# The order of the products in a blocked triangular inverse: both Y of a pair of steps, then both Z

## The reference, cut to what matters

```python
kb = k * beta[..., None]
a_mat = jnp.where(strict, jnp.einsum("bhnid,bhnjd->bhnij", kb, k) * decay, 0.0)
rhs = jnp.concatenate([v * beta[..., None], kb * jnp.exp(gc)[..., None]], axis=-1)
sol = lax.linalg.triangular_solve(a_mat + eye, rhs, left_side=True, lower=True,
                                  unit_diagonal=True)
...
def step(s, inp):
    u_n, w_n, qk_n, qd_n, kt_n, gt_n = inp
    v_new = u_n - jnp.einsum("bhck,bhkv->bhcv", w_n, s)
    o = jnp.einsum("bhck,bhkv->bhcv", qd_n, s) + jnp.einsum("bhcj,bhjv->bhcv", qk_n, v_new)
    s = s * gt_n[..., None, None] + jnp.einsum("bhck,bhcv->bhkv", kt_n, v_new)
    return s, o
```

## Time and profile before

| what | value |
|---|---|
| median of three executions | 3063.61 us |
| the profiled execution, its own time | 3054.48 us |
| its span, first to last instruction | 3052.8 us |
| mean granted TensorE clock, share of full speed | 0.939 |
| TensorE matmuls busy, over the span | 2665.8 us (87%) |
| VectorE / ScalarE / GpSimd busy | 1777.7 / 1232.9 / 1169.0 us |
| chunk stage, inverse and state, 1758 to 2742 us | 984 us |

### The profile page before, as it was taken

How to read it: one execution, slowest core, us unless ns; L and a number is a source line. 1 busy time by engine, 2 the same in 40 slices (tenths; PEclk the granted TensorE clock), 3 DMA queues, 4 the chain that set the end, 5 groups by cost and what they waited for, 6 DMA issues and landing times. The chain is left out here.

```text
span 3052.8 us, 52964 instructions
## 1 busy us (share of the span) xinstructions
PE 2665.8 (87%) x18657; PEld 2562.7 (84%) x18657; DVE 1777.7 (58%) x2689; ACT 1232.9 (40%) x2107; POOL 1169.0 (38%) x1110
## 2 busy tenths in 40 slices
PE   4799999984997299999999799999999999994994
PEld 3799999974996299999999799998998999994993
DVE  2266666666102357778777756766666666664004
ACT  2255555554112244444444434454554544443101
POOL 3333333322220134545444344455545455543220
PEclk9899999997998599999999889999999999997996
DMA  3111111113112035555554352424234243214103
GB/s 114 49 50 57 58 57 52 57 50 128 67 41 112 20 96 150 137 151 158 151 158 143 112 157 45 117 49 109 74 83 109 46 108 108 52 37 160 49 27 111
DMA packets 244802, 275.54 MB, mean 90 GB/s; under 512 B 86907, under 2 KB 210380, under 8 KB 242972
## 3 DMA queue, kind: packets, MB, share of 16 engines
q1 hardware_dynamic: 240028, 256.31, 29.5%
q10 hardware_dynamic: 4608, 17.04, 1.4%
HBM read 185.78 MB, written 87.53 MB: 90 GB/s over the span
## 5 line engine op out<-in xcount | busy, mean ns | idle before, releaser
L1895 ACT ACTIVATE zz<-ps 104x416 fp32r<-104x416 f32 x560 | 286.5, 518 | 379.8 <-PE ps L1786 378.4
L551 PE MATMUL ps<-dn_yhi,dn_whi 128*128 128x416 f32 (+1 forms) x1152 | 395.4, 343 | 18.5 <-POOL dn_wlo L535 13.1
L1958 DVE TENSOR_TENSOR pp<-ps,level_mask 104x416 fp32r<-104x416 f32 x560 | 318.3, 585 | 114.5 <-PE ps L1786 113.9
L552 PE MATMUL ps<-dn_ylo,dn_whi 128*128 128x416 f32 (+1 forms) x1152 | 376.1, 326 | 0.0
L553 PE MATMUL ps<-dn_yhi,dn_wlo 128*128 128x416 f32 (+1 forms) x1152 | 376.0, 326 | 0.0
L551 PE MATMUL ps<-rg_yhi,rg_whi 128*128 128x416 f32 (+1 forms) x768 | 256.2, 334 | 57.5 <-POOL rg_wlo L535 36.9
L1788 PE MATMUL ps<-pp,zz 104*104 104x208 f32 x1440 | 264.2, 293 | 18.4 <-DVE pp L1958 16.0
L552 PE MATMUL ps<-rg_ylo,rg_whi 128*128 128x416 f32 (+1 forms) x768 | 255.2, 332 | 0.0
L553 PE MATMUL ps<-rg_yhi,rg_wlo 128*128 128x416 f32 (+1 forms) x768 | 254.2, 331 | 0.0
L1788 PE MATMUL ps<-zz,pp 104*104 104x208 f32 x1440 | 245.1, 280 | 0.0
L551 PEld LDWEIGHTS ps<-dn_yhi,dn_whi 128*128 128x128 f32 x1152 | 218.9, 190 | 25.0 <-POOL dn_wlo L535 13.5
(11 more groups left out here) (283 smaller groups left out, 7311.3 us busy)
## 6 DMA issues: line engine op xcount, KB each, us to landing
c_nq<-nq_scratch SPq DMA_DIRECT2D x160, 169.0 KB
dn_raw<-in_dn_w_in SPq DMA_DIRECT2D x48, 512.0 KB, 4.0
qd<-rows_scratch SPq DMA_DIRECT2D x160, 104.0 KB, 3.3
rg_raw<-in_rg_w_in SPq DMA_DIRECT2D x32, 512.0 KB, 4.0
nq_scratch<-p_nq SPq DMA_DIRECT2D x48, 338.0 KB
p_ex<-rows_scratch SPq DMA_DIRECT2D x32, 422.5 KB
nq_scratch<-p_rn SPq DMA_DIRECT2D x32, 338.0 KB
o_scratch<-a SPq DMA_DIRECT2D x16, 520.0 KB, 2.8
```

What stands on the lines that cost most here:

```text
L551: e.matmul(o, whi, mhi[:, t0:t0 + tn], start=(first and k == 0), stop=False)
L552: e.matmul(o, whi, mlo[:, t0:t0 + tn], start=False, stop=False)
L1895: e.activation(zz[:, b, :, :], ps[0:CH, 2 * b + 1, 0:m4], ACT.Copy).then_inc(zev.sem, 1)
L1958: e.tensor_tensor(D4(pp[:, b, l % 2, :, :]), D4(Y4), c["level_mask"][:, l, :, 0:CH].unsqueeze(2).to_broadcast([CH, 2, 2, CH]), ALU.mult).t ...
```

## The change

In slots 1 to 7, TensorE no longer does Y and Z of the first step and then Y and Z of the second. The call for the first step does nothing; the call for the second does Y of both steps and then Z of both. What each group computes, where it reads and writes, what it waits for and which semaphore it raises are as before. Slots 0, 8 and 9 move into `ends` and keep their order. The other engines' programs are the same, and the counts of `ym` and `zm` come in the same order within each semaphore.

```diff
@@ dn_chunks, block.tensor, make(n)
                 def inverse(g, l):
-                    b, q4 = g % 2, g % 4
+                    if not 1 <= l <= LEVELS:
+                        ends(g, l)
+                    elif g % 2:
+                        for side in (grow_y, grow_z):
+                            side(g - 1, l)
+                            side(g, l)
+
+                def grow_y(g, l):
+                    b = g % 2
+                    old, p_ = nhr[:, g % 4] if l == 1 else zz[:, b], pp[:, b, (l - 1) % 2]
+                    e.wait_ge(yev.sem, yev.at(n, nth(g, l - 1, YS)))
+                    if l >= 2:
+                        e.wait_ge(zev.sem, zev.at(n, nth(g, l - 2, LEVELS)))
+                    for m in MS:
+                        ins = widened(2 * b, m, old[:, m, :], p_[:, m, :])
+                    ins.then_inc(ym.sem, 1)
+
+                def grow_z(g, l):
+                    b = g % 2
+                    old, p_ = nhr[:, g % 4] if l == 1 else zz[:, b], pp[:, b, (l - 1) % 2]
+                    if l == 1 and g >= 2:
+                        e.wait_ge(tb_done.sem, tb_done.at(n, g - 1))
+                    for m in MS:
+                        ins = widened(2 * b + 1, m, p_[:, m, :], old[:, m, :])
+                    ins.then_inc(zm.sem, 1)
+
+                def ends(g, l):
...
-                    elif l <= LEVELS:
-                        old, p_ = nhr[:, q4] if l == 1 else zz[:, b], pp[:, b, (l - 1) % 2]
-                        e.wait_ge(yev.sem, yev.at(n, nth(g, l - 1, YS)))
-                        if l >= 2:
-                            e.wait_ge(zev.sem, zev.at(n, nth(g, l - 2, LEVELS)))
-                        for m in MS:
-                            ins = widened(2 * b, m, old[:, m, :], p_[:, m, :])
-                        ins.then_inc(ym.sem, 1)
-                        if l == 1 and g >= 2:
-                            e.wait_ge(tb_done.sem, tb_done.at(n, g - 1))
-                        for m in MS:
-                            ins = widened(2 * b + 1, m, p_[:, m, :], old[:, m, :])
-                        ins.then_inc(zm.sem, 1)
```

More of the change, by code:

```diff
@@ L1799, in inverse @@
                         for m in MS:
-                            ins = widened(2 * b, m, nhr[:, q4, m, :], ident_r[:, :])
+                            ins = widened(2 * b, m, nhr[:, g % 4, m, :], ident_r[:, :])
                         ins.then_inc(ym.sem, 1)
-                    elif l <= LEVELS:
-                        old, p_ = nhr[:, q4] if l == 1 else zz[:, b], pp[:, b, (l - 1) % 2]
-                        e.wait_ge(yev.sem, yev.at(n, nth(g, l - 1, YS)))
-                        if l >= 2:
-                            e.wait_ge(zev.sem, zev.at(n, nth(g, l - 2, LEVELS)))
-                        for m in MS:
-                            ins = widened(2 * b, m, old[:, m, :], p_[:, m, :])
-                        ins.then_inc(ym.sem, 1)
-                        if l == 1 and g >= 2:
-                            e.wait_ge(tb_done.sem, tb_done.at(n, g - 1))
-                        for m in MS:
-                            ins = widened(2 * b + 1, m, p_[:, m, :], old[:, m, :])
-                        ins.then_inc(zm.sem, 1)
                     elif l == LEVELS + 1:
```

## The result

The changed kernel takes 3086.2 us in the median (3084.26 to 3090.51), the kernel before, beside it, 3061.31 us: a ratio of 1.0085, 95% interval 1.0068 to 1.0103, or **24.9 us slower**. The forecast was 3077.1, with 3072 to 3083 as its own range and 3066 to 3090 with the rivals. Two more comparisons gave 1.0076 (1.0060 to 1.0092) and 1.0102 (1.0073 to 1.0132). The profiled execution has 3085.98 us with a span of 3084.3.

What follows compares the result with a forecast made beforehand. TensorE's queue was taken to set the chunk stage's pace, with no slack in the zz loop. Terms 9.1 + 2.0 + 2.4 = 13.5 us, added to the median 3063.6, gave 3077.1 us; own range 3072 to 3083, with rivals 3066 to 3090.

Steps and rivals of the forecast that it cites:

- the clock rival: Added stops in the chunk stage tip four undisturbed table periods into lower clock: 12 us more, about 3089 us; chance 0.08.
- The loop Y0, Z0, eviction, Y0: TensorE to ScalarE and back: 1.15 us from Z0 to next Y0, no slack; a bare level grows from 1.55 to 1.93.
- 9.1 + 2.0: Boundary 4 to 5: 24 bare cases at 0.38 us, plus 40 at 0.05 for Y1 behind paired ScalarE evictions.
- The covers: TensorE's state pieces after levels 2, 3, 5 and 7, each over 0.43 us, hide the loss there.
- the 0.46 of L1878: L1878's matmuls, after level 1 in three periods of five and level 6 in two, just hide the loss.
- no gain on VectorE: Y1 reaches VectorE 0.38 us earlier, but rr waits for TensorE's state product after 0.70 idle, so zero gain.
- taken back: Rival: VectorE waits at 6 to 7 swallow most of the 4 to 5 loss, leaving 5.7 us (3069); chance 0.10.
- the pairs: Second of two successive evictions delays Y1 by 0.05 us: 2.0 us in all on ScalarE, 2.4 on VectorE.
- Periods 26.1 and 23.6: Sign: chunk-stage periods of 25.5 and 23.0 us become 26.1 and 23.6.
- Those with the square within 0.1: Sign: periods where ScalarE does the output's square (L1908) ahead of zz stay within 0.1 us.
- TensorE's waits for zz up by 9 to 11: Sign: the sum of TensorE's zz waits rises about 9 to 11 us, some written to the weight loads.
- Waits for VectorE near 31: Sign: TensorE's waits for VectorE, 28.9 us before, stay near 29 plus 2.

Runs made afterwards that it cites:

- Level 4 alone: Changed kernel with both Y before both Z kept only in level 4, other levels in the old order: 3070.26 us, 1.0035 against the kernel before.
- level 3 alone: Changed kernel with both Y before both Z kept only in level 3: 3057.21 us against 3059.25 for the kernel before, ratio 0.9995.
- levels 2, 3 and 5: Changed kernel with both Y before both Z kept only in levels 2, 3 and 5: 3072.12 us, ratio 1.0045 to the kernel before.
- late tables: VectorE's four table operations moved behind the inverse's slot 7: 3064.4 us on the changed kernel, 3047.8 in the old order, 3042.66 there with scalings later too.
- level 5 alone: Changed kernel with both Y before both Z kept only in level 5: 3073.7 us, ratio 1.0053 to the kernel before.

## Why the prediction was right, and where it was off

The direction and the mechanism were right, the size was not: 13.5 us were forecast and 24.9 measured. 3086.2 lies above the forecast's own range, which ends at 3083, and inside the wide one only because that reached up to the clock rival. Some 16 us are the forecast's mechanism; the rest is mostly clock, to which it gave 0.08.

**Right: the bound and the place.** The loop Y0, Z0, eviction, Y0 had no slack; with one more group in it the level at 4 to 5 is 1.93, as computed. Level 4 alone costs 10 us, where the sum had 9.1 + 2.0 for this boundary. The covers held: level 3 alone costs nothing, and the 0.46 of L1878 hid what it was to hide (A and B grow by 0.10 and 0.14, not by 0.4). What the prediction did not look at is the entry of a level: Y1, moved earlier, has its own bare side at 4 to 5, which levels 2, 3 and 5 showed. In the full change it falls on the same boundary, so the sum did not suffer; that was luck.

**Right: no gain on VectorE.** rr is released by the state product; the early Y evictions only lengthened the idle time ahead of it, from 0.70 to 0.99. The waits of 0.30 and 0.86 at 6 to 7 are 0.31 and 0.88 now, so nothing was taken back.

**Mis-sized: the pairs.** The offsets from the period's start, medians of the two traces, show the parts. In C, D and E, level 4 starts 0.09 later than before; levels 4 and 5 add 0.36 to 0.39; levels 6 and 7 add 0.11 to 0.13. So the second of a ScalarE pair cost next to nothing, not 0.05. The second of a VectorE pair cost 0.12 at 6 to 7, not 0.05: Y1 came 0.50 after Y0, where I had 0.47, and I had left out that the group after it takes 0.42 in place of 0.38. At the levels' start the same happens at 0 to 1 in all 40 periods, where I had counted it for the 8 first of a head alone; it leaves 0.09 in C, D and E, and A and B are 0.12 longer in all. Summed: 24 x (0.09 + 0.38 + 0.12) + 16 x 0.12 = 16.1 us, against 13.5. The stage's start, where the first period runs at 1.2 GHz, I had not counted; its first two periods are 1.3 and 1.1 us longer with late tables.

**Mis-sized: the clock.** The rival "the clock falls more often" had 0.08 and a price of 12 us. It came true in part beside the forecast. The sum of 39 periods is 957 to 961 us before and 987 to 988 after, 29 apart; with 16 for the order and 1.7 for the start, some 11 are left. About six of these are new falls: 7 in three traces, mostly at 2.7 us each (28.8 in place of 26.1). The rest are falls that both kernels have and that cost more in the changed one: the 4th period takes 30.4 us at a granted clock of 0.83, where it took 28.2 to 28.5 at 0.88, and the 24th 31.1 to 32.7, where it took 27.7 to 28.2. The prediction had asked only how often the clock falls, not for how long. By the medians (24.9) the clock's part is about 7. Three of its readings there don't hold. It counted 8 periods with the tables, 4 of them undisturbed; there are 7, and 3 were. It spoke of hundreds of short stops at full clock; the earlier trace rows have 65. And that waits of 0.86 cost no clock in the D periods was beside the point: the question was what a stop of 1.57 does when more short stops surround it. The sentence on the Trainium skill there (TensorE: Matmul & The Clock Gate, "A second HAM failure mode: psum-queue depth-cycling") speaks of a clock that swings because of short stops between groups. Here, the three kernels with late tables, whose stops at the tables are 0.34 to 0.94, kept full clock in these periods, and all falls in them came behind a stop of 1.1 to 1.8.

**Signs foretold.** Periods 26.1 and 23.6: measured 26.1 and 23.57. Those with the square within 0.1: 0.10 and 0.14. A wait of 0.35 to 0.40 for zz at 4 to 5: shown as 0.23, with the starts 0.38 apart from before. TensorE's waits for zz up by 9 to 11: up by 12.2, plus 18.8 on the weight loads, part of it the same time. Waits for VectorE near 31: 23.0, as those at 1 to 2 are now put down to zz (0.31), which comes a little later there than pp. And one of the signs that it had named for being wrong was there: periods at a clock below 1 grew in number, in the five E periods from 2 or 3 to 4 or 5.

**Still open.** Why the full new order raises the share of falls when level 4 or level 5 alone doesn't, and why the clock stays low longer in the 4th and the 24th period. With late tables the 24th takes 28.8 in the new order and 28.4 in the old, so its excess seems to hang on the early tables as well; but one trace of each is little, and in the old order with late tables the 14th took 30.9.

## What to carry to other kernels

When two chains share an engine and each group's result comes back through another engine, count the groups that lie between a group's end and its next use: here 1.15 us of loop stood against groups of 0.38, and taking one group out of the gap cost one group, 0.36 to 0.39 us, at the one boundary (4 to 5) without other work. Moving a group earlier can cost as much as moving one later, since it comes nearer to what it reads; so a boundary must be covered on both sides, and a "harmless" subset (levels 2, 3 and 5) has to be checked at its entry too. A single long stop can be worth more than its length if the clock falls behind it. Moving four small VectorE operations out of it gave 11.5 us. By estimate from the traces, the stop itself is about half of this (five periods at 25.5 - 24.3 = 1.2 us each), and 2 to 3 falls of the clock at some 3 us the rest.

## What the runs showed of the hardware that was not expected

A VectorE copy or scaling of 104 x 40 takes 0.17 to 0.18 us, but mostly 1.04 to 1.05 when it comes 0.1 us after the start of a GpSimd multiplication of 1.11 us, and both then end within 0.05 of each other. This was so in 39 of the 44 E periods (9th, 19th, 29th, 34th) of the eleven traces with early tables; in the other 5 the small one took 0.18 and GpSimd's 1.21, and TensorE's stop was 0.70 instead of 1.57. The copy just before it, which starts 0.02 after GpSimd's, is not held. Late tables do not take this away: in the old order with late tables head_eg takes 0.17 in all eight heads, but in its E periods head_tail takes some 0.86 and head_beta 1.05, beside GpSimd's uu, where TensorE does not wait for them. The Trainium skill (GPSIMD Engine Reference, "1. Specifications") says that GpSimd shares its interfaces to SBUF with VectorE and that they contend under certain conditions; the rows fit that, and show that the one that loses waits for the whole of the other. What makes it lose was not isolated.

And in the E periods the clock does not fall in the long stop but behind it, while TensorE is busy again: in the 9th period of the changed kernel the granted clock is still 1.00 in the first 1 us behind the stop and 0.50 from 1967.2 on.
